# The first layer's two attentions: from 32 units of one kind each to 16 steps of one unit of each kind

## Chip, core and metric

The kernel runs on one core of one Trainium2 chip. The metric is the device time of one execution in microseconds (us), the median of several runs. The engines are called PE (TensorE; PEld is its weight load), DVE (VectorE), ACT (ScalarE), POOL (GpSimd) and SP (SyncE, which here only issues DMAs).

## What is computed

Two transformer blocks on one sequence of 512 tokens of 1024 features. The change touches the first one: two of its four mixers, and the second part of its modulation.

```python
# differential attention, 4 heads, two score maps of 32 features each ("kind A")
s = einsum('bqhcd,bkhcd->bhcqk', q, k) * 32 ** -0.5
p = softmax(s, axis=-1)
a = p[:, :, 0] - lam * p[:, :, 1]
o = rmsnorm(einsum('bhqk,bkhd->bqhd', a, v), subln_g) * (1.0 - lam_init)
# neighbourhood attention, 4 heads of 64 features, biased window + context ("kind B")
p = softmax(concatenate([s_win + bias, s_ctx], axis=-1), axis=-1)
# modulation: silu(c) @ ada_w + ada_b; four of the six parts are needed only behind the attentions
x = x + g1 * (concatenate([a_out, b_out, pool_out, hyena_out], axis=-1) @ w_out)
```

Both attentions have 512 queries (4 tiles `t` of 128) and 768 keys (256 of the context, 512 of the sequence), all in float32.

## The kernel before

The program is written engine by engine. `plan()` lists every PSUM product in the order in which PE makes it, with its banks; a product's banks are waited for (`fill`), its end is counted (`done`, waited for by `ready`), and its reader frees its first bank (`bank_free`, waited for by `read`). Each engine works through its own list in the order in which the code is written, so any wait holds back all that is written behind it. Weight tiles of 512 KB go through a ring of 12 slots; SP loads them in the order of use, each as soon as the slot's last reader has counted (`begun`, or `mod_read` for a tile of the modulation).

The attentions are one stage between the mixers' projections (`projections`) and the output product (`first_out`, `w_out`). `UNITS` are 32 units: first 16 of kind A (head by head, tile by tile), then 16 of kind B. For unit `i`, PE makes scores (L961), 6 transposes of the probabilities (L981) and 6 products with the values (L989, "PV"; values as weights, 64 columns, probabilities moving). DVE takes the row maxima (L1915, for B the bias first, L1914), the reciprocal of the row sums (L1931), normalises the probabilities (L1934 to L1938), copies the result of the unit before (L1923, `take_o`), and adds one term of the second modulation, a ring tile times a column of `silu(c)` (`mod_terms`, L1742 and L1748; 32 terms, one with each unit). ACT takes the exponentials with their sums (L1499) and copies the transposed probabilities (L1419). Scores have two pairs of banks in turn (0 and 1, 2 and 3); those of unit i+1 stand before the transposes of unit i.

Ahead of the first unit DVE prepares masks, bias and lambda (L1886 to L1905). Behind the last unit stand the 32 products that sum the modulation over the partitions (L997), and the norm of kind A's heads over all tokens (L1004, L1411, L1414, L1947).

Of the kernel before, what the change touches and what calls it, by code (L numbers as in the profile page):

```python
# [14 lines left out]
P = 128  # L15
# [163 lines left out]
def plan():  # L179
# [21 lines left out]
    r["mod2"] = b.take(7)  # L201
    b.order -= 1
    pair = 0
    for i in range(-1, len(UNITS)):
        if i + 1 < len(UNITS):
            r["scores", i + 1] = []
            for _ in range(2 if UNITS[i + 1][0] == "A" else 1):
                r["scores", i + 1].append(b.take(2 * pair, 2 * pair + 1))
                pair = 1 - pair
        if i >= 0:  # L210
            r["T", i] = [b.take(4), b.take(5)]
            r["PV", i] = b.take(6)
    r["mod2"].order = b.order
    b.order += 1
    r["subln"] = [b.take(4), b.take(5)]

    r["before_w_out"] = b.settle()
# [46 lines left out]
UNITS = [(a, h, t) for a in "AB" for h in range(HEADS) for t in range(ST)]  # L264
# [32 lines left out]
for _name, _n in (("ms_x", 1), ("ms_c", 1), ("subln", 2), ("ms_2", 1), ("ms_f", 1), ("ms_ab", 2), ("qk_ms", 10),  # L297
                  (("ffn_ms", 0), 2), ("ms_ret", 2), (("ffn_ms", 1), 1)):
    _made += _n
    ROOTS[_name] = _made  # L300


MIXED_1 = 4
MIXED_2 = MIXED_1 + 4


def two_blocks(nc, d):
# [5 lines left out]
    with ExitStack() as ctx:  # L313
# [65 lines left out]
        unused_row = tiny[:, 425:426]  # L379

# [36 lines left out]
        o_a = piece(arena, 8192, 2, S)  # L417
        prob = piece(arena, 9216, 2, 2, NKEY)
        prob_t = piece(arena, 12288, 2, NKT, P)
        raw_a = piece(arena, 13824, 4, S)  # L420
        prob_sq = piece(arena, 13824, 2, S)
        sub_rs_t = arena[:, 14848:15872]
        acc2 = piece(h_flat, D, 4, TILE)
        pool_u = piece(arena, 9216, 2, S + 16)
# [77 lines left out]
        mod_read = sem("modulation_tiles_read")  # L502
        done = sem("products_done")
# [18 lines left out]
        max_ready, exp_ready, prob_ready = sem("max_ready"), sem("exp_ready"), sem("prob_ready")  # L522
        bias_set, lam_arg, lam_exp = sem("bias_set"), sem("lam_arg"), sem("lam_exp")
        sub_sq = sem("o_a_squares")
# [85 lines left out]
        def _(sp):  # L610
# [3 lines left out]
            def read_by(t):  # L614

                if t < mod1_end:
                    return mod_read, t + 1
                if t < mod2:
                    return begun, t - mod1_end + 2
                if t < mod2_end:  # L620
                    return mod_read, 16 + t - mod2 + 1
                return begun, t - mod1_end - 32 + 3

            def load(n):

                if n >= RING:
                    sem_, value = read_by(n - RING)
                    sp.wait_ge(sem_, value)
                sp.dma_start(ring[:, n % RING, :], d["weights"][n]).then_inc(landed[n % RING], 16)

            def stream(first, last):

                turns = (last - first) // RING
                if turns:
                    with sp.Fori(0, turns) as it:
                        for s in range(RING):
                            n = first + s
                            sem_, value = read_by(n - RING)
                            sp.wait_ge(sem_, it * RING + value)
# [45 lines left out]
        def _(pool):  # L685
# [10 lines left out]
            pool.dma_start(dft, d["dft_half"]).then_inc(dft_in, 16)  # L696

# [56 lines left out]
        def _(pe):  # L754
# [192 lines left out]
            def attentions():  # L947
                def scores(i):
                    kind, h, t = UNITS[i]
                    for c, p in enumerate(r["scores", i]):  # L950
                        fill(p)
                        if kind == "A":
                            o, n, q, k = 64 * (h % 2) + 32 * c, 32, aq, ak
                            if i == 0 and c == 0:
                                pe.wait_ge(roped, 4)
                                read(pe, r["ak"][3])
                                read(pe, r["ak"][1])
                        else:
                            o, n, q, k = 64 * (h % 2), 64, bq, bk
                        for at, width in ((0, 512), (512, 256)):  # L960
                            m = pe.matmul(wide(p, NKEY)[:, at:at + width], q[o:o + n, h // 2, t * P:(t + 1) * P],  # L961
                                          k[o:o + n, h // 2, at:at + width], start=True, stop=True)
                            if i == 0 and c == 0 and at == 0:
                                begin(m)
                        finish(p, m)

                read(pe, r["bq"][1])
                for j in range(4):
                    read(pe, r["bk"][j])
                for j in range(NKT):  # L970
                    read(pe, r["v"][j])
                fill(r["mod2"])
                scores(0)
                for i, (kind, h, t) in enumerate(UNITS):
                    if i + 1 < len(UNITS):
                        scores(i + 1)
                    pe.wait_ge(prob_ready, i + 1)
                    for j, p in enumerate(r["T", i]):
                        fill(p)
                        for kt in range(4 * j, min(4 * j + 4, NKT)):  # L980
                            m = pe.transpose(ps[:, p.bank, (kt % 4) * P:(kt % 4 + 1) * P], prob[:, i % 2, 0, kt * P:(kt + 1) * P], ident)  # L981
                        finish(p, m)
                    p = r["PV", i]
                    fill(p)
                    o = DH * (h % 2)
                    for kt in range(NKT):
                        if kt % 4 == 0:
                            read(pe, r["T", i][kt // 4])
                        m = pe.matmul(ps[o:o + DH, p.bank, 0:P], vals[:, kt, 0 if kind == "A" else 1, h * DH:(h + 1) * DH],  # L989
                                      prob_t[:, i % 2, kt, :], start=(kt == 0), stop=(kt == NKT - 1))  # L990
                    finish(p, m)

                p = r["mod2"]
                for i in range(32):
                    if i % 8 == 0:
                        pe.wait_ge(mod_read, 16 + i + 8)
# [4 lines left out]
                for c, p in enumerate(r["subln"]):  # L1001
                    fill(p)
                    pe.wait_ge(sub_sq, 1)
                    finish(p, pe.matmul(bank(p), head_ones, prob_sq[:, c], start=True, stop=True))  # L1004

            def first_out():
                for b, v in r["before_w_out"]:
                    pe.wait_ge(bank_free[b], v)
                pe.wait_ge(mixed, MIXED_1)
                for i in range(8):  # L1010
# [386 lines left out]
        def _(act):  # L1397
# [91 lines left out]
            def attentions():  # L1489
# [3 lines left out]
                unit = [0]  # L1493

                def exps(i):
                    for c, p in enumerate(r["scores", i]):
                        unit[0] += 1
                        act.wait_ge(max_ready, unit[0])
                        act.activation(prob[:, i % 2, c], wide(p, NKEY), ACT.Exp, bias=neg_max[:, i % 2, c:c + 1],  # L1499
                                       accum_out=row_sum[:, i % 2, c:c + 1]).then_inc(bank_free[p.bank], 1)  # L1500

                exps(0)
                for i in range(len(UNITS)):
# [1245 lines left out]
```

## Time and profile before

| | before |
|---|---|
| median of 3 runs | 2761.19 us (2760.93 to 2763.34) |
| profiled execution, its own time | 2758.17 us |
| span of its profile | 2756.0 us |
| PE busy | 2551.9 us (93%) |
| DVE / ACT / POOL busy | 966.8 / 527.0 / 65.1 us |
| last product before the attentions to first product of `w_out` | 335.48 to 549.98 us of the span |

The span is the time between the first and the last record of the profile; the time of an execution holds some 2 us more. A busy share is an average over stages with different limits: this program is serial from stage to stage, so the stage of the attentions is read by itself. A float32 product shows as two records of PE. "idle before <-releaser" in a row says how long the engine stood still before it, and who ended that.

### The profile page before, as it was taken

How to read it: one execution, taken by the hardware profiler on the slowest of the kernel's cores; microseconds unless marked ns; L12 is line 12 of the kernel's file. 1: busy time of each engine (PE TensorE's matmuls, PEld its weight loads, DVE VectorE, ACT ScalarE, POOL GpSimd, SP SyncE). 2: the span in 40 equal slices, each digit the busy share in tenths (PEclk: the TensorE clock that was granted, in tenths of full speed). 3: DMA queues.
4: the chain of work that ended last, by engine and by line, in shares of the span. 5: the costliest groups of instructions: out<-in, count | busy, mean ns of one | idle time of the engine just before them, and what ended most of it. 6: DMA issues, size and time to landing. Idle time of an engine off the chain costs nothing.

```text
span 2756.0 us, 31092 instructions
## 1 busy us (share of the span) xinstructions
PE 2551.9 (93%) x11540; PEld 1924.5 (70%) x11540; DVE 966.8 (35%) x1743; ACT 527.0 (19%) x1095; POOL 65.1 (2%) x163
## 2 busy tenths in 40 slices
PE   7999977787999996977989999989999989899999
PEld 3565455546888884864778888847657668788888
DVE  7231277522000003126253443333323443534432
ACT  2200043321112113154121110012122110221100
POOL 1000000000111110000000000000000000000000
PEclk9999978896999997987999999999999999999999
DMA  9202123105999894210222222221211202222221
GB/s 328 99 8 62 54 72 90 54 0 193 331 329 333 327 329 179 69 31 1 62 69 77 91 79 75 91 100 54 82 48 53 76 24 105 79 92 85 84 82 63
DMA packets 83346, 307.12 MB, mean 111 GB/s; under 512 B 9264, under 2 KB 9264, under 8 KB 82624
## 3 DMA queue, kind: packets, MB, share of 16 engines
q1 hardware_dynamic: 75888, 274.24, 29.7%
q0 software_dynamic: 7376, 31.77, 2.9%
q8 instruction: 55, 0.90, 0.1%
q14 instruction: 27, 0.22, 0.0%
HBM read 292.86 MB, written 13.11 MB: 111 GB/s over the span
## 4 chain that ended last, share of the span: by engine, by line
PE 87%; DVE 7%; ACT 3%; issue 2%; DMA 1%; SPq 0%; DVEq 0%; POOL 0%; ACTq 0%; POOLq 0%
PE products L1197 37%; PE products L788 12%; PE products L1078 9%; PE products L942 7%; PE products L1090 4%; PE products L989 2%; PE products L961 2%; PE products L1323 2%; PE products L1267 1%; PE products L852 1%; PE products L896 1%; PE products L906 1%; PE products L803 1%; PE products L1181 1%; PE products L1311 1%
## 5 line engine op out<-in xcount | busy, mean ns | idle before, releaser
L1197 PE MATMUL products<-normed,ring 128*128 128x264 f32 (+1 forms) x1312 | 303.9, 388 | 11.3 <-DVE normed L2289 11.3
L1197 PEld LDWEIGHTS products<-normed,ring 128*128 128x128 f32 x1312 | 252.1, 193 | 56.1 <-issue 16.0
L1419 ACT ACTIVATE arena<-products 128x264 f32<-128x264 f32 (+3 forms) x263 | 118.6, 468 | 729.8 <-PE products L788 203.0
L1078 PEld LDWEIGHTS products<-arena,ring 128*128 128x128 f32 x2176 | 248.3, 194 | 8.8 <-issue 8.8
L1078 PE MATMUL products<-arena,ring 128*128 128x128 f32 x2176 | 248.6, 277 | 0.8 <-ACT arena L1534 0.8
L788 PE MATMUL products<-normed,ring 128*128 128x264 f32 (+2 forms) x736 | 219.7, 462 | 3.5 <-DVE normed L1726 3.5
L788 PEld LDWEIGHTS products<-normed,ring 128*128 128x128 f32 x736 | 141.6, 193 | 81.5 <-issue 65.6
L942 PE MATMUL products<-ring,normed 128*128 128x512 f32 (+1 forms) x416 | 182.5, 599 | 8.4 <-DVE normed L1726 8.4
L1197 PE MATMUL products<-arena,mixed 128*128 128x256 f32 (+1 forms) x832 | 189.4, 382 | 0.0
L1197 PEld LDWEIGHTS products<-arena,mixed 128*128 128x128 f32 x832 | 158.1, 190 | 23.8
L1197 PE MATMUL products<-normed,mixed 128*128 128x264 f32 (+1 forms) x704 | 161.5, 383 | 0.0
L1197 PE MATMUL products<-arena,normed 128*128 128x264 f32 (+1 forms) x704 | 155.6, 383 | 0.0
L942 PEld LDWEIGHTS products<-ring,normed 128*128 128x128 f32 (+1 forms) x416 | 73.7, 178 | 115.8 <-issue 115.8
L1197 PEld LDWEIGHTS products<-normed,mixed 128*128 128x128 f32 x704 | 133.8, 190 | 20.5
L1197 PEld LDWEIGHTS products<-arena,normed 128*128 128x128 f32 x704 | 133.8, 190 | 20.5
L2078 DVE TENSOR_TENSOR arena<-products,arena 128x512 f32<-128x512 f32 x17 | 11.7, 691 | 371.1 <-PE products L1078 371.1
L1197 PE MATMUL products<-arena,ring 128*128 128x256 f32 (+1 forms) x544 | 121.1, 382 | 1.6 <-DVE arena L2436 1.4
L1090 PE MATMUL products<-ring,arena 128*128 128x512 f32 x272 | 121.3, 599 | 0.0
L788 PE MATMUL products<-mixed,ring 128*128 128x264 f32 (+1 forms) x384 | 114.2, 460 | 6.2 <-DVE tiny L1952 5.3
L1197 PEld LDWEIGHTS products<-arena,ring 128*128 128x128 f32 x544 | 103.2, 190 | 18.0 <-DVE arena L2436 1.8
L788 PEld LDWEIGHTS products<-mixed,ring 128*128 128x128 f32 x384 | 73.5, 192 | 47.5 <-issue 39.3
L989 PE MATMUL products<-arena 128*64 128x128 f32 x384 | 62.8, 328 | 38.4 <-DVE arena L1923 20.3
(424 smaller groups left out, 2827.9 us busy)
## 6 DMA issues: line engine op xcount, KB each, us to landing
ring<-in_weights SPq DMA_DIRECT2D x303, 512.0 KB, 4.1
ring<-in_experts SPq DMA_DIRECT2D x204, 512.0 KB, 5.0
arena<-results SPq DMA_DIRECT2D x8, 512.0 KB, 7.6
residual<-in_x POOLq DMA_DIRECT2D x1, 2048.0 KB, 16.2
arena<-in_dft_half POOLq DMA_DIRECT2D x1, 2048.0 KB, 8.4
token_rows<-arena SPq DMA_DIRECT2D x4, 512.0 KB, 2.9
out<-residual SPq DMA_DIRECT2D x8, 256.0 KB, 4.6
arena<-in_bias POOLq DMA_DIRECT2D x1, 1920.0 KB, 24.5
```

The lines of the kernel that those rows point to most:

```text
L788: m = pe.matmul(bank(p, n), w[:, k, :], acts[:, k, at:at + n], start=(k == 0), stop=(k == kt - 1))
L803: m = pe.matmul(bank(p, n), ones, sq[:, k, at:at + n], start=(k == 0), stop=(k == KT - 1))
L852: m = pe.matmul(bank(p), w[:, c, tt, :], filt[:, tt, :, 0, :] if c == 0 else diff[:, tt], start=(tt == 0), stop=(tt == ST - 1))
L896: m = pe.matmul(ps[:, p.bank, c * 256:(c + 1) * 256], dft[:, c, tt, kt * P:(kt + 1) * P], sig_t[:, tt], start=(tt == 0), stop=(tt == ST - 1))
L942: m = pe.matmul(ps[0:n_tok, p.bank, :], acts(k), w[k // 2][:, k % 2, :], start=(k == 0), stop=(k == KT - 1))
L961: m = pe.matmul(wide(p, NKEY)[:, at:at + width], q[o:o + n, h // 2, t * P:(t + 1) * P], k[o:o + n, h // 2, at:at + width], start=True, sto ...
L989: m = pe.matmul(ps[o:o + DH, p.bank, 0:P], vals[:, kt, 0 if kind == "A" else 1, h * DH:(h + 1) * DH], prob_t[:, i % 2, kt, :], start=(kt = ...
L1078: m = pe.matmul(ps[:, side, m_ * P:(m_ + 1) * P], w[:, k, :], job_t[:, k, :], start=(k == 0), stop=(k == KT - 1))
L1090: m = pe.matmul(ps[:, 4 + half, :], hid[:, k, :], ring[:, s, half * 512:(half + 1) * 512], start=(k == 0), stop=(k == 3))
L1197: m = pe.matmul(bank(p, n), left(k), right(k), start=(fresh and k == 0), stop=(k == kt - 1), skip_group_check=True)
L1323: m = pe.matmul(ps[:, p.bank, at:S], ret_v[0:n, t, i * P:(i + 1) * P], ret_s[0:n, t, at:S], start=(t == 0), stop=(t == 4), skip_group_chec ...
L1419: act.activation(out, src, ACT.Copy, scale=scale).then_inc(bank_free[p.bank], 1)
```

## The change

The units are regrouped in 16 steps `(t, h)`. Step `s` holds the unit of kind A for head `h` and the unit of kind B for head `h ^ 1`, so that the scores of A read rows 0-63 of the array (two maps of 32 rows) and those of B rows 64-127, or the other way round. Kind A's two score maps lie side by side in banks 0, 1 and 2, kind B's in 3 and 4, transposes in 5 and 6, PV in 7: each has one set instead of two in turn. PV now has the probabilities as weights and the values moving, so that its result is token-major, 128x64; ACT copies it out and multiplies by the reciprocal row sum on the way, so that DVE no longer normalises kind B and combines kind A in one operation. The head norm is done tile by tile (`head_squares`, `roots`, `head_norm`) and the result transposed by PE (`feature_major`). The odd terms of the second modulation go to POOL, in two operations each, a product and a sum. DVE's preparation stands before the pool mixer's last products. The host stacks the modulation tiles in the new order of use.

```diff
+    scores(0, "A")
+    scores(0, "B")
+    for s in range(len(STEPS)):
+        scores(s + 1, "A")
+        scores(s + 1, "B")
+        turned(s, "A")
+        weighed(s - 1, "B")
+        turned(s, "B")
+        weighed(s, "A")
+        if s in OUT_AT:
+            r["OT", OUT_AT[s]] = [b.take(5), b.take(6)]
...
-UNITS = [(a, h, t) for a in "AB" for h in range(HEADS) for t in range(ST)]
+STEPS = [(t, h) for t in range(ST) for h in range(HEADS)]
+OUT_AT = {HEADS * t + 5: t for t in range(ST - 1)}
...
 SP, read_by:
-                    return mod_read, 16 + t - mod2 + 1
+                    j = t - mod2
+                    return (mod_added, j // 2 + 1, RING // 2) if j % 2 else (mod_read, 16 + j // 2 + 1, RING // 2)
...
 POOL:
+            ready(pool, r["scores", 0, "A"])
+            for j in range(1, 32, 2):
...
+                    pool.tensor_scalar(mod_term, w, silu_c[:, k, 0:1], None, ALU.mult).then_inc(mod_scaled, 1)
+                    pool.wait_ge(mod_scaled, j // 2 - part + 2)
+                    pool.tensor_tensor(acc2[:, part], acc2[:, part], mod_term, ALU.add).then_inc(mod_added, 1)
+                pool.wait_ge(mod_added, j // 2 + 1)
...
 PE, scores of kind A:
+                        for c, at, key, width in ((0, 0, 0, 512), (1, NKEY, 0, 256), (1, 1024, 256, 512), (0, 512, 512, 256)):
+                            rows_ = slice(o + 32 * c, o + 32 * c + 32)
+                            if at == 512:
+                                pe.wait_ge(half_scored, s + 1)
...
 PE, weigh:
-                        m = pe.matmul(ps[o:o + DH, p.bank, 0:P], vals[:, kt, 0 if kind == "A" else 1, h * DH:(h + 1) * DH],
-                                      prob_t[:, i % 2, kt, :], start=(kt == 0), stop=(kt == NKT - 1))
+                        m = pe.matmul(ps[:, p.bank, 0:DH], prob_t[:, a, kt, :], vals[:, kt, a, h * DH:(h + 1) * DH],
+                                      start=(kt == 0), stop=(kt == NKT - 1))
...
 PE, order of a step, and behind the last:
+                    scores(s + 1, "A")
+                    scores(s + 1, "B")
+                    turn(s, "A")
+                    if s > 0:
+                        weigh(s - 1, "B")
+                    turn(s, "B")
+                    weigh(s, "A")
...
+                pe.wait_ge(mod_read, 16 + 16)
+                pe.wait_ge(mod_added, 16)
...
+                feature_major(ST - 1)
...
 ACT:
+                for s in range(len(STEPS)):
+                    turned(s, "A")
+                    if s > 0:
+                        weighed(s - 1, "B")
+                    exps(s + 1, "A")
+                    turned(s, "B")
+                    exps(s + 1, "B")
+                    weighed(s, "A")
+                    if s % HEADS == 0 and s > 0:
+                        roots(s // HEADS - 1)
+                    if s in OUT_AT:
+                        feature_major(OUT_AT[s])
+                weighed(len(STEPS) - 1, "B")
+                roots(ST - 1)
+                feature_major(ST - 1)
...
 DVE:
+                def joined(s):
+                    read(dve, r["scores", s, "A"])
+                    link(dve.reciprocal(inv[:, 0:2], sums[:, 0:2]))
+                    link(stt(inv[:, 1:2], inv[:, 1:2], neg_lam, sums[:, 0:1], ALU.mult, ALU.mult))
+                    stt(prob_a[:, 0], prob_a[:, 1], inv[:, 1:2], prob_a[:, 0], ALU.mult, ALU.add).then_inc(prob_ready, 1)
...
+                for s in range(len(STEPS)):
+                    joined(s)
+                    if s in OUT_AT:
+                        head_norm(OUT_AT[s])
+                    maxima(s + 1, "A")
+                    if s % HEADS == 0 and s > 0:
+                        head_squares(s // HEADS - 1)
+                    mod2_term(2 * s)
+                    read(dve, r["scores", s, "B"])
+                    dve.reciprocal(row_inv[:, s % 2, 2:3], row_sum[:, s % 2, 2:3]).then_inc(inv_b, 1)
+                    maxima(s + 1, "B")
+                head_squares(ST - 1)
+                head_norm(ST - 1)
```

On PE this is one inner unit of kind A before (`arena` holds queries, keys, values and probabilities, `products` the PSUM banks; 128x512 and 128x256 are scores):

```order
L961 MATMUL products<-arena 128x512
L961 MATMUL products<-arena 128x256
L961 MATMUL products<-arena 128x512
L961 MATMUL products<-arena 128x256
L981 MATMUL products<-const_sb,arena 128x128 x6
L989 MATMUL products<-arena 64x128 x6
```

And this is the first part of an inner step on PE after the change, with the semaphores that each row waits for (`bank_free_0` is freed by the exponentials of kind A, `bank_free_3` by those of kind B, 5 and 6 by ACT's copies of the transposes, 7 by ACT's copy of PV):

```order
L1002 MATMUL products<-arena 128x512 [waits bank_free_0]
L1002 MATMUL products<-arena 128x256
L1002 MATMUL products<-arena 128x512
L1002 MATMUL products<-arena 128x256 [waits bank_of_both_score_halves_written]
L1010 MATMUL products<-arena 128x512 [waits bank_free_3]
L1010 MATMUL products<-arena 128x256
L1023 MATMUL products<-const_sb,arena 128x128 [waits bank_free_5,prob_ready]
L1023 MATMUL products<-const_sb,arena 128x128 x3
L1023 MATMUL products<-const_sb,arena 128x128 [waits bank_free_6]
L1023 MATMUL products<-const_sb,arena 128x128
L1034 MATMUL products<-arena 128x64 [waits bank_free_5,bank_free_7]
```

The scores of both kinds of step s+1 (L1002 and L1010) now stand before kind A's transposes of step s (L1023), with the wait for kind B's bank between them; behind the last row come kind B's transposes and kind A's PV.

On ACT, the same step after the change (128x64 is a copy of PV, 128x768 an exponential, 128x512 and 128x256 are copies of transposes):

```order
L1493 ACTIVATE arena<-products 128x512 [waits products_done]
L1493 ACTIVATE arena<-products 128x256 [waits products_done]
L1493 ACTIVATE arena<-products,tiny 128x64 [waits products_done,row_inverse_b]
L1575 ACTIVATE arena,tiny<-products,tiny 128x768 [waits max_a]
L1575 ACTIVATE arena,tiny<-products,tiny 128x768
L1493 ACTIVATE arena<-products 128x512 [waits products_done]
L1493 ACTIVATE arena<-products 128x256 [waits products_done]
L1575 ACTIVATE arena,tiny<-products,tiny 128x768 [waits max_b]
L1493 ACTIVATE arena<-products,tiny 128x64 [waits products_done]
```

Before, ACT's list for a unit held only the two copies of transposes and then the exponentials of the next unit. Now the exponential of kind B, which frees bank 3, stands behind those of kind A and behind the copies of kind B's transposes.

## Rows read from the trace of the kernel before

**Rows 1.** The page of the profile: the chain that ended last, by engine.

```profile
PE 87%; DVE 7%; ACT 3%; issue 2%; DMA 1%; SPq 0%; DVEq 0%; POOL 0%; ACTq 0%; POOLq 0%
```

**Rows 2.** Windows around and in the stage; columns as in their first line.

```profile
core 0: us, PE busy (x) PEld busy (x) DVE busy (x) ACT busy (x) POOL busy (x), PEclk, DMA share, GB/s
...
345.00:445.00 100.00, 76.97 (x392) 53.49 (x393) 80.59 (x127) 41.38 (x94) 0.00 (x0) 0.79 0.26 77
...
460.00:532.00 72.00, 53.74 (x320) 37.14 (x319) 54.01 (x86) 28.39 (x60) 0.00 (x0) 1.00 0.27 81
```

**Rows 3.** Timeline of the stage's start: us, us long, engine, line, operation.

```profile
336.54 1.61 DVE L1882 TENSOR_SCALAR mixed<-products,small 128x512 f32<-128x512 f32 x2 [30.52 <-PE products L936]
...
338.62 1.65 PE L961 MATMUL products<-arena 32*128 32x512 f32 x8 [1.25 <-DVE mixed L1882]
...
345.40 1.82 DVE L1915 TENSOR_REDUCE tiny<-products 128x1 f32<-128x768 f32 x2
```

**Rows 4.** Timeline of one unit of kind A at full clock.

```profile
360.71 0.17 DVE L1931 RECIPROCAL tiny<-tiny 128x2 f32<-128x2 f32 x1
...
360.90 1.56 PE L961 MATMUL products<-arena 32*128 32x512 f32 x8
...
361.76 1.02 DVE L1936 SCALAR_TENSOR_TENSOR arena<-arena,tiny 128x768 f32<-128x768 f32 x1
...
362.69 1.81 DVE L1915 TENSOR_REDUCE tiny<-products 128x1 f32<-128x768 f32 x2
362.83 0.64 PEld L981 LDWEIGHTS products<-const_sb,arena 128*128 128x128 f32 x6 [0.77 <-DVE arena L1936]
...
363.52 0.87 ACT L1419 ACTIVATE arena<-products 128x512 f32<-128x512 f32 x2 [2.92 <-PE products L981]
364.28 0.91 ACT L1499 ACTIVATE arena<-products,tiny 128x768 f32<-128x768 f32 x1
...
364.62 1.27 DVE L1748 SCALAR_TENSOR_TENSOR normed<-ring,tiny,normed 128x1024 f32<-128x1024 f32 x1
...
364.75 1.52 PE L989 MATMUL products<-arena 128*64 128x128 f32 x12 [1.05 <-DVE arena L1923]
...
365.94 0.22 ACT L1499 ACTIVATION_READ_ACCUMULATOR arena<-products,tiny 128x1 f32 x1
...
366.26 0.17 DVE L1931 RECIPROCAL tiny<-tiny 128x2 f32<-128x2 f32 x1 [0.37 <-ACT arena L1499]
```

**Rows 5.** The chain that ended last, through one unit of kind B.

```profile
466.20 1.52 PE products L989 x12
467.72 1.50 PE products L961 x4
...
469.25 0.71 DVE products L1914
...
471.18 1.52 PE products L989 x12
```

**Rows 6.** Timeline of the stage's end.

```profile
531.37 1.28 ACT L1411 ACT_TABLE_LOAD   x1
...
531.70 9.33 PE L997 MATMUL products<-const_sb,normed 128*128 128x1 f32 x64
...
549.98 10.25 PE L788 MATMUL products<-mixed,ring 128*128 128x512 f32 x19 [5.32 <-DVE tiny L1952]
```

**Rows 7.** The chain that ended last, in kind A where the granted clock was lower.

```profile
382.73 2.55 PE products L989 x12
385.28 2.10 PE products L961 x8
```

**Rows 8.** Groups by line and shape: ACT, then POOL. Columns: busy us, mean ns.

```profile
L1419 ACT ACTIVATE arena<-products 128x256 f32<-128x256 f32 x32 | 12.1, 378 | 0.0
...
L704 POOL TENSOR_TENSOR tiny<-const_sb 128x1 f32<-128x1 f32 x71 | 13.9, 196 | 220.8 <-PE products L1064 217.6
```

More of the change, by code:

```diff
@@ L198, in plan, with scores, turned, weighed @@
         r[name] = b.many(n)
[L201 to L217, printed above, removed]
+    def scores(s, kind):
+        if s < len(STEPS):
+            r["scores", s, kind] = b.take(0, 1, 2) if kind == "A" else b.take(3, 4)
+    def turned(s, kind):
+        r["T", s, kind] = [b.take(5), b.take(6)]
+    def weighed(s, kind):
+        if s >= 0:
+            r["PV", s, kind] = b.take(7)
+    scores(0, "A")
[10 more added lines that the diff above has]
+    weighed(len(STEPS) - 1, "B")
+    r["mod2"] = b.take(0)
+    r["OT", ST - 1] = [b.take(5), b.take(6)]
+    b.turn = 1
     r["w_out"] = b.many(8)
@@ new lines, in turn @@
+                def turn(s, kind):
+                    of = prob_a[:, 0] if kind == "A" else prob_b
+                    if kind == "A":
+                        pe.wait_ge(prob_ready, s + 1)
+                    else:
+                        read(pe, r["scores", s, "B"])
+                    for j, p in enumerate(r["T", s, kind]):
+                        fill(p)
+                        for kt in range(4 * j, min(4 * j + 4, NKT)):
+                            m = pe.transpose(ps[:, p.bank, (kt % 4) * P:(kt % 4 + 1) * P], of[:, kt * P:(kt + 1) * P], ident)
+                        finish(p, m)
@@ L1000, in attentions @@
                 tile_no[0] += 32
[L1001 to L1004, printed above, removed]
+                feature_major(ST - 1)
             def first_out():
-                for b, v in r["before_w_out"]:
-                    pe.wait_ge(bank_free[b], v)
                 pe.wait_ge(mixed, MIXED_1)
+                for p in r["pool_w"] + r["OT", ST - 1]:
+                    read(pe, p)
                 for i in range(8):
@@ new lines, in roots, with feature_major @@
+                def roots(t):
+                    act.wait_ge(sub_sum, t + 1)
+                    act.activation(sub_ln, sub_ms, ACT.Ln, bias=eps, scale=1.0 / DH).then_inc(sub_logs, 1)
+                    act.wait_ge(sub_logs, t + 1)
+                    act.activation(sub_rs, sub_ln, ACT.Exp, scale=-0.5).then_inc(sub_root, 1)
+                def feature_major(t):
+                    for a, p in enumerate(r["OT", t]):
+                        copy(p, mix[:, 2 * a:2 * a + 2, t * P:(t + 1) * P], bank(p, 2 * P).rearrange("p (c q) -> p c q", c=2),
+                             sub_g if a == 0 else 1.0)
```

262 lines of the change are left out of this document (146 added, 116 removed).

## Prediction

> **What bounds the kernel now.** I read the page first: its chain [rows 1] lies almost wholly on PE, and the program goes from stage to stage, so what this stage loses or gains passes on to the end. The windows [rows 2] then show that the stage of the attentions is different: PE is busy for 76.97 of 100 us among kind A's units and 53.74 of 72 us among kind B's, DVE for 80.59 and 54.01. Neither is full, so I read single units.
>
> A unit of kind A at full clock [rows 4] lasts from one reciprocal (360.71) to the next (366.26), 5.55 us. DVE's rows there, with the two small ones between them, come to 5.3 us with gaps of some 0.03 us: DVE bounds kind A. A unit of kind B [rows 5] lasts from 466.20 to 471.18, 4.98 us, and its chain goes round: PV, scores, DVE's bias, its maxima and its copy of the last PV, which PE waits for before it may write the bank again. DVE and PE take turns. The granted clock is 0.79 over kind A and 1.00 over kind B [rows 2]. With slower units at the low clock (PV 2.55 us for 1.52, scores 2.10 for 1.56 [rows 4, 7]) the 32 units take from 345.40 [rows 3] to about 531.8, the start of the modulation's products [rows 6]: 186 us, or 11.65 us for a pair of one A and one B.
>
> At the start PE's first scores begin at 338.62, but DVE takes up their maxima only at 345.40, behind its preparation [rows 3]. At the end 18.3 us pass from 531.70 to `w_out`'s first product at 549.98: 9.33 us of modulation products, then sums, two roots with a table load each, and two DVE operations [rows 6].
>
> **The start.** DVE stood idle 30.52 us before the pool mixer's last two operations [rows 3], which hides the 7 us of preparation once it stands ahead of them; if it were not hidden, it would cost what it cost before. The first scores still wait for those operations and start at 338.6. They end at 340.3, the maxima (one operation over 2x768; two cost 1.81 [rows 4]) at 342.1, the two exponentials (1.88 us from the first start to the accumulator's end [rows 4]) at 344.0. Step 0 has no PV of the step before; its probabilities are ready at 345.6, transposed and copied at 348.4, and the exponentials of A in step 1 end at 350.3.
>
> **An inner step.** Call e the end of kind A's exponentials of a step. Work per step, from [rows 4, 5, 8]:
> DVE: reciprocals and a small operation 0.50, join 1.02, maxima of A 1.81, modulation term 1.27, bias 0.70, maxima of B 0.91, eight gaps 0.25: 6.5 us, and 0.25 for the tile's head norm (three operations of 256 columns in four steps, estimated from the 768-column rows). 6.75 us.
> ACT: two pairs of copies 0.87 each, exponentials 1.88 and 1.0, two PV copies of 0.25 each (below the 0.378 us of the 256-column copy): 5.1 us.
> PE: scores 1.56 and 1.50, transposes 0.64 twice, PV twice. PV now loads 128 columns of weights instead of 64 and moves 64 instead of 128. No row has that shape; the transposes' weight loads go at 0.64/6 = 0.107 us each, the old PV at 1.52/12 = 0.127. I take 0.107, as loads will set the pace: 1.28 us. The upper end, the modulation products' 9.33/64 = 0.146 us at a mixed clock [rows 6], gives 1.75. Sum: 6.9 us.
>
> So no engine needs more than 6.9 us. But one set of banks for each kind ties them into a ring. From e, ACT first copies kind B's transposes (0.87), then takes kind B's exponential (1.0): bank 3 is free at e+1.9. PE made the scores of A at e+0.1 to 1.6 meanwhile; those of B start only now, so **the scores of the two kinds do not run side by side** in an inner step, whatever rows they use. They end at e+3.4. Behind them in PE's queue stand kind A's transposes, though their probabilities have been ready since e+1.5: done at e+4.0; PV of B at e+5.3, seen by ACT at e+5.6. ACT's copy of PV stands before the next exponentials of A: those run from e+5.8 to e+7.7. **7.7 us for a pair at full clock**, with DVE idle for 1 us and PE for 0.8.
>
> At the low clock this ring gets longer by 0.6 to 1.3 (scores of B), 0.3 (transposes) and 0.9 (PV): near 10 us [rows 4, 7]. PE would be busy 90% of a step, more than in either half now, of which the less busy, B, kept 1.00; but kind A's 32-row scores, which went with 0.79, stay. I take the middle, 0.90: a fifth of the time at low clock, 8.15 us a step. The ends are 7.7 and 8.7.
>
> **The tiles' ends.** Three times ACT loads two tables (1.28 each [rows 6]) and takes two short functions of 0.2: 3.0 us, from e+2.2 to e+5.2, where its next copy is due at e+4.1. That copy and the PV copy slip, the exponentials by about 0.5: 1.5 us for the three. Without the slack in the ring they would cost 9.
>
> **POOL's terms.** Nothing in the trace shows POOL on such a tile. Below, a product and a sum cost no less than DVE's two-input row, 1.27 us; above, POOL has about 8 us for a term, since it takes the odd tiles one for each step. DVE can run ahead by six tiles, the half of the ring that POOL holds; SP's queue loads in order, so a late term of POOL holds back DVE's tiles too, and PE's products wait for all 16 sums. At 3 us a term, between those ends and nearer the DVE row, all of it is hidden. The Trainium skill (GPSIMD Engine Reference, section 3.1) gives 4497 ns for an addition of 2048 float32 a partition against VectorE's 2293; by that estimate a term would be 3 to 4 us, and the sum would not change. No run here shows it yet.
>
> **The end of the stage.** After the last e (step 15) DVE's join is ready at e+1.6; transposes, PV of B, transposes, PV of A, PV of B follow on PE without a wait: e+6.7. The modulation's 64 records take 6.9 us at 0.107 and took 9.33 with the clock falling; I take 8.0. The last tile's head norm (copies, squares, 3.0 us of roots) ends before that. Four transposes, their lag and two copies of 0.38 add 1.5: `w_out` starts at e+16.2.
>
> **Sum.** 350.3 + 14 x 8.15 = 464.4 for the e of step 15, + 1.5 + 16.2 = 482.1, where it was 549.98. That is 68 us less. Nothing behind it changes. The profiled execution's 2758.17 us would become 2690; against the median of 2761.19, 3 us above it, **2693 us**. The ends of 7.7 and 8.7 us move this by 6.3 and 7.7 us; with 1.5 either way for PV's price and the end, the forecast's own range is 2685 to 2703. **0.68.**
>
> **Rivals.**
> *The scores do overlap, or ACT's order costs less than I think* (kind B's exponential done soon after e). Then DVE's 6.75 us bounds the step: 14 x 1.4 = 20 us less, 2673. For it: DVE did bound kind A. Against: the place of kind B's exponential in ACT's queue. **0.09.**
> *DVE and POOL hold each other up at SBUF.* If each of DVE's two two-input operations on SBUF in a step (1.02 and 1.27 us) waits for one operation of POOL, at least 1.27 us long, DVE needs 6.75 + 2.54 = 9.3 us and becomes the bound: 14 x 1.15 = 16 us more, 2709. It decides only past the 1 us that DVE idles in a step, and needs POOL busy at each such moment. **0.12.** The Trainium skill (SBUF — State Buffer, on the shared port pair) says just this of a DVE operation with two SBUF inputs and a reading GpSimd operation: the later one waits for the whole of the earlier. No row of before can show it, since POOL only has one-column operations there [rows 8].
> *The clock stays low throughout*, about 10 us a step: 14 x 1.85 = 26 us more, 2719. Against it stands the dense PE. **0.08.**
> *POOL is the bound and the kernel gets slower.* PE's products and what follows take 9.5 us, POOL starts at 340.3: at (550 - 9.5 - 340.3)/16 = 12.5 us a term the gain is gone; at 15 us it is 40 us slower, 2801. That is ten times DVE's row. **0.03.**
>
> **How the numbers follow.** The likeliest case gives the time. Forecast, first rival and second rival hold 0.89; the range runs from 2676, most of the first, to 2714, past the second. A measurement of this kernel can tell about 0.2% (5.5 us) from no change; all cases but the last are far beyond: faster 0.96, same 0.01, slower 0.03.
>
> **What would show it.** In the changed profile: an inner step of 7.7 us at clock 1.00; scores of B starting 1.8 us or more after those of A and right behind ACT's exponential of B; ACT's exponentials of A right behind its PV copy; DVE with some 1 us idle in a step; DVE's 1.27 us and 1.02 us rows no longer than before (else the second rival); the last POOL sum before the last PV; `w_out` near 482. I would be wrong if PE's new PV went well above 1.75 us, or if table loads or POOL stretched more than three steps.

## The result: slower, and the profile after

The changed kernel takes 2787.01 us (median of 20 runs, 2760.12 to 2793.89); the kernel before, run beside it 20 times, 2760.31 us. The ratio is 1.0085, with a 95% interval of 1.0065 to 1.0104. I had forecast 2693 us, a range of 2676 to 2714, and a chance of 0.96 for faster. The profiled execution has a span of 2784.7 us, 28.7 more than before. Ratios leave out executions recorded as slow: three of ten of "The tile's transposes moved, narrow PV" (2782 to 2785 us) and one of six of "The same with wide PV" (3709.31 us), while medians hold all.

The page of the changed kernel, parts 1 and 2:

```profile
PE 2630.6 (94%) x11552; PEld 1994.2 (72%) x11552; DVE 928.8 (33%) x1657; ACT 542.3 (19%) x1144; POOL 145.1 (5%) x193
...
PEclk9999955586999998996999999999999999999999
```

The clock's digits show it: three slices at 5, from 348 to 557 us, where the attentions are (the kernel before has 7, 8, 8 there; the 6 two slices on stood there before too). The windows of the changed kernel (columns as in the first line) answer to [rows 2]:

```profile
core 0: us, PE busy (x) PEld busy (x) DVE busy (x) ACT busy (x) POOL busy (x), PEclk, DMA share, GB/s
345.00:445.00 100.00, 99.64 (x338) 72.88 (x339) 50.72 (x63) 38.58 (x91) 60.80 (x23) 0.50 0.21 74
445.00:560.00 115.00, 115.00 (x418) 89.16 (x417) 50.45 (x72) 48.67 (x113) 15.55 (x6) 0.50 0.19 64
```

PE is busy nearly all the time, and its clock is at the lower level, 1.2 GHz, throughout; before it was 0.79 among kind A's units and 1.00 among kind B's from 460 us on. One step on PE, from the timeline of the changed kernel (it answers to [rows 4, 5, 7]):

```profile
412.17 3.37 PE L1002 MATMUL products<-arena 32*128 32x512 f32 x8
415.47 2.92 PE L1010 MATMUL products<-arena 64*128 64x512 f32 x4
418.32 1.54 PE L1023 MATMUL products<-const_sb,arena 128*128 128x128 f32 x6
419.66 2.66 PE L1034 MATMUL products<-arena 128*128 128x64 f32 x12
422.11 1.49 PE L1023 MATMUL products<-const_sb,arena 128*128 128x128 f32 x6
```

From start to start these are 3.30, 2.85, 1.34, 2.45 and 1.28 us (the second PV starts at 423.39), and a second PV of about 2.5 follows: 13.7 us, back to back. DVE's join of the steps 1, 3, 4 and 15, which now waits for ACT each time:

```profile
354.94 0.17 DVE L2038 RECIPROCAL tiny<-tiny 128x2 f32<-128x2 f32 x1 [1.97 <-ACT arena L1575]
...
383.09 0.17 DVE L2038 RECIPROCAL tiny<-tiny 128x2 f32<-128x2 f32 x1 [3.17 <-ACT arena L1575]
396.90 0.17 DVE L2038 RECIPROCAL tiny<-tiny 128x2 f32<-128x2 f32 x1 [4.34 <-ACT arena L1575]
...
551.41 0.17 DVE L2038 RECIPROCAL tiny<-tiny 128x2 f32<-128x2 f32 x1 [4.34 <-ACT arena L1575]
```

An inner step takes 13.81 us (383.09 to 396.90). The stage's end answers to [rows 6]: 

```profile
577.10 0.90 PEld L1044 LDWEIGHTS products<-const_sb,arena 128*128 128x128 f32 x4
...
578.01 0.47 ACT L1493 ACTIVATE mixed<-products,tiny 128x256 f32<-128x256 f32 x1 [10.58 <-PE products L1044]
...
579.18 2.04 PE L829 MATMUL products<-mixed,ring 128*128 128x512 f32 x2 [0.78 <-ACT mixed L1493]
```

`w_out` starts at 579.18; it was 549.98, and I had put it at 482.1. The 29.2 us between the kernels are the difference of the spans (28.7) to within 0.5 us.

### The profile page after: what moved, and what is told of

Its sections match the earlier page's. It is cut to its first block, busy times and chain, and to the rows that moved or that the text cites. A ratio compares the mean times of both kernels' runs of the same rounds, so it can differ in the third digit from the quotient of the medians.

```text
span 2784.7 us, 31110 instructions
## 1 busy us (share of the span) xinstructions
PE 2630.6 (94%) x11552; PEld 1994.2 (72%) x11552; DVE 928.8 (33%) x1657; ACT 542.3 (19%) x1144; POOL 145.1 (5%) x193
## 4 chain that ended last, share of the span: by engine, by line
PE 90%; DVE 5%; ACT 2%; issue 1%; DMA 1%; SPq 0%; DVEq 0%; POOL 0%; ACTq 0%; POOLq 0%
PE products L1271 37%; PE products L829 12%; PE products L1152 9%; PE products L983 7%; PE products L1164 4%; PE products L1034 3%; PE products L1002 2%; PE products L1397 2%; PE products L1023 2%; PE products L1010 2%; PE products L1341 1%; PE products L893 1%; PE products L937 1%; PE products L844 1%; PE products L947 1%
## 5 line engine op out<-in xcount | busy, mean ns | idle before, releaser
L2201 DVE TENSOR_TENSOR arena<-products,arena 128x512 f32<-128x512 f32 x17 | 11.7, 691 | 371.0 <-PE products L1152 371.0
L829 PE MATMUL products<-mixed,ring 128*128 128x264 f32 (+1 forms) x384 | 114.1, 460 | 1.7 <-DVE mixed L2296 0.9
L1164 PEld LDWEIGHTS products<-ring,arena 128*128 128x128 f32 x272 | 50.3, 190 | 61.0 <-issue 56.9
```

What stands on the lines that cost most here:

```text
L829: m = pe.matmul(bank(p, n), w[:, k, :], acts[:, k, at:at + n], start=(k == 0), stop=(k == kt - 1))
L1164: m = pe.matmul(ps[:, 4 + half, :], hid[:, k, :], ring[:, s, half * 512:(half + 1) * 512], start=(k == 0), stop=(k == 3))
```

## The experiments

All were timed beside the kernel before on the same chip; ratios are to it, with their 95% intervals. Theory 1 was that PV's new operand order keeps the clock low, theory 2 that the rest of the dense step does, theory 3 that POOL and DVE block one another. "Narrow" PV is the changed kernel's, with 64 moving columns; "wide" PV moves 128. The diffs show the lines that matter, cut to length.

**PV with 128 moving columns.** Same weights, the values of two heads past them, half of the result read.

```diff
-  m = pe.matmul(ps[:, p.bank, 0:DH], prob_t[:, a, kt, :], vals[:, kt, a, h * DH:(h + 1) * DH], ...
+  m = pe.matmul(ps[:, p.bank, 0:P], prob_t[:, a, kt, :], vals[:, kt, a, (h - h % 2) * DH:(h - h % 2 + 2) * DH], ...
```

> The changed kernel, but each PV product moves the values of two heads (128 columns for 64) past the same weights; 64 of the 128 result columns are read. Theory 1 (the new PV, which loads 128 columns of weights for 64 moving columns, is what keeps the clock at 0.50): the clock in the stage rises above 0.9, a step takes 7.7 to 8.7 us, the kernel about 2695 to 2710 us. Theory 2 (the clock is low because of the rest of the step, the 32-row scores and the transposes in a dense row, whatever PV does): clock 0.50, a step of 13.8 us as in the changed kernel, 2787 us.

2712.89 us, ratio 0.9813 (0.9785 to 0.9841). One edit (ACT's copy picks its half of the columns with it) turns 0.85% slower into 1.9% faster, by making PE move more. Windows of this kernel:

```profile
345.00:445.00 100.00, 92.57 (x486) 66.83 (x487) 72.82 (x89) 56.02 (x133) 75.12 (x28) 0.84 0.33 106
...
375.00:385.00 10.00, 9.84 (x64) 7.36 (x64) 9.13 (x12) 5.58 (x14) 9.72 (x4) 1.00 0.31 105
```

Theory 1 holds over theory 2, though the clock is 0.84 where it expected above 0.9, and the time 3 us above its range: the clock is 1.00 in the inner steps and falls at the tiles' ends. This kernel's joins, in inner steps at full clock and then around a tile's end:

```profile
372.45 0.17 DVE L2038 RECIPROCAL tiny<-tiny 128x2 f32<-128x2 f32 x1 [1.19 <-ACT arena L1575]
380.20 0.17 DVE L2038 RECIPROCAL tiny<-tiny 128x2 f32<-128x2 f32 x1 [0.26 <-ACT arena L1575]
387.95 0.17 DVE L2038 RECIPROCAL tiny<-tiny 128x2 f32<-128x2 f32 x1
400.34 0.15 DVE L2038 RECIPROCAL tiny<-tiny 128x2 f32<-128x2 f32 x1
411.06 0.17 DVE L2038 RECIPROCAL tiny<-tiny 128x2 f32<-128x2 f32 x1 [4.12 <-ACT arena L1575]
```

An inner step is 7.75 us at clock 1.00; the step with a tile's end takes 12.39, and the next 10.72. What holds up the tile's end in this kernel:

```profile
392.92 0.88 DVE L2051 TENSOR_TENSOR arena<-arena,tiny 128x256 f32<-128x256 f32 x1 [3.50 <-ACT tiny L1596]
...
395.51 0.90 ACT L1575 ACTIVATE arena<-products,tiny 128x768 f32<-128x768 f32 x1 [1.61 <-DVE tiny L2026]
...
398.01 0.99 PE L1044 MATMUL products<-const_sb,arena 128*128 128x128 f32 x4 [2.31 <-ACT arena L1493]
```

DVE waits 3.50 us for ACT's roots before its head norm (L2051); the maxima of kind A stand behind that in DVE's list, ACT's exponentials wait for the maxima, ACT's copies of kind B's transposes stand behind the exponentials, and PE waits for the banks that those copies free.

**PV's old operand order in the new steps**, values as weights again, results used as they lie.

```diff
+  m = pe.matmul(ps[0:DH, p.bank, 0:P], vals[:, kt, a, h * DH:(h + 1) * DH], prob_t[:, a, kt, :], ...
```

> The changed kernel with PV's operands as they were before: values as weights (64 columns), probabilities moving (128 columns). Its result then lies feature by token and is copied and used as if it were token by feature, so the attention part of the output is not the reference's; durations are those of the full work. Theory 1: clock above 0.9 and about 2700 us, as in the run with wide PV. Theory 2: clock 0.50 and 2787 us or a little more, since the old form took 2.55 us for one product set at low clock and the new one 2.66.

2716.86 us, ratio 0.9832 (0.9802 to 0.9861), clock 0.88 from 345 to 445 us and 0.92 from there to 532. 64 weight columns here, 128 in the run before, 128 moving columns in both, and the same effect: the moving side matters.

**The kernel before, with PV swapped alone.**

```diff
+  m = pe.matmul(ps[:, p.bank, 0:DH], prob_t[:, i % 2, kt, :], vals[:, kt, 0 if kind == "A" else 1, h * DH:(h + 1) * DH], ...
```

> The kernel before with PV's operands swapped alone (probabilities as weights, 64 columns of values moving); the attention result is taken from the wrong places, so the output is not the reference's. Theory 1: the clock falls to 0.5 in both halves of the stage (it was 0.79 and 1.00), and the kernel takes 30 to 60 us more than before. Theory 2: the clock stays near 0.79 and 1.00 and the time within 10 us of before, rather less, since a set of PV products gets shorter at full clock (1.28 for 1.52 us).

2828.58 us, ratio 1.0241 (1.0213 to 1.0268): 66 us more than before from this line alone. Windows of this kernel; they were at 0.79 and 0.96 in the kernel before. PE was less busy here than in the changed kernel (89.58 of 100 us for 99.64), and the clock is 0.50 all the same:

```profile
345.00:445.00 100.00, 89.58 (x320) 61.45 (x320) 65.77 (x104) 33.59 (x77) 0.00 (x0) 0.50 0.21 63
445.00:532.00 87.00, 80.29 (x258) 55.59 (x256) 47.53 (x74) 22.33 (x51) 0.00 (x0) 0.50 0.23 67
```

**POOL's terms back on DVE**, narrow PV.

```diff
   mod2_term(2 * s)
+  mod2_term(2 * s + 1)
```

> The changed kernel with POOL's 16 terms of the modulation back on DVE, two terms in each step. Theories 1 and 2: PE is the bound at 0.50, DVE idles some 7 us of each 13.8 us step and takes 1.3 us more; 2787 us within 5. Theory 3 (POOL and DVE blocking one another at SBUF costs the step): faster than the changed kernel by more than 10 us.

2788.92 us, ratio 1.01 (1.0075 to 1.0124), as the changed kernel. Theory 3 falls as the cause. One of the five executions took 2760.43 us, and that one was profiled: its clock is at 1.00 from 355 to 378 us and then falls to 0.50 for the rest of the attentions. Two windows and PE's rows of one step at full clock (L987 are kind A's scores, L1008 transposes, L1019 the narrow PV):

```profile
362.00:378.00 16.00, 15.57 (x100) 11.53 (x99) 14.64 (x20) 10.01 (x27) 0.00 (x0) 1.00 0.43 139
404.00:450.00 46.00, 46.00 (x155) 33.26 (x153) 24.43 (x32) 17.65 (x40) 0.00 (x0) 0.50 0.20 69
...
360.61 1.89 PE L987 MATMUL products<-arena 32*128 32x512 f32 x8 [0.21 <-ACT arena L1559]
...
364.62 1.45 PE L1019 MATMUL products<-arena 128*128 128x64 f32 x12
365.91 0.83 PE L1008 MATMUL products<-const_sb,arena 128*128 128x128 f32 x6
...
368.30 1.89 PE L987 MATMUL products<-arena 32*128 32x512 f32 x8 [0.21 <-ACT arena L1559]
```

With the narrow PV an inner step at full clock is 7.69 us (360.61 to 368.30) and a PV 1.29 (364.62 to 365.91). PE was busy for 15.57 of the 16 us ahead of the fall; from 378 to 388 the clock is 0.54 with PE busy for all 10 us.

**The same with wide PV.**

> Wide PV (128 moving columns), and POOL's 16 modulation terms back on DVE. With the clock up, POOL and DVE hold each other up in the wide kernel: DVE's 1.27 us term took 1.63 on average and up to 3.37. Theory A (that blocking costs more than half the terms are worth): at full clock DVE needs 6.75 + 1.3 = 8.05 us a step against the ring's 7.75, but the steps at the tiles' ends get shorter; about 2705 to 2713 us, no slower than the wide kernel (2713). Theory B (the blocking is hidden and the 1.3 us are not): 14 steps of 0.3 to 1.3 us more, 2717 to 2730 us.

2709.33 us, ratio 0.9815 (0.9791 to 0.9838); wide PV with POOL had 0.9813. No difference that can be told for the kernel. The first tile's end is shorter, as theory A had it (10.73 and 7.29 us for 12.39 and 10.72), and some inner steps are longer (8.53 for 7.75).

**The finished tile's transposes moved**, wide PV. They go from the end of step 5 into step 6, between PV of B and kind B's transposes, on PE, on ACT and in `plan()`.

```diff
-OUT_AT = {HEADS * t + 5: t for t in range(ST - 1)}
+OUT_AT = {HEADS * t + 6: t for t in range(ST - 1)}
...
                     if s > 0:
                         weigh(s - 1, "B")
+                    if s in OUT_AT:
+                        feature_major(OUT_AT[s])
                     turn(s, "B")
                     weigh(s, "A")
-                    if s in OUT_AT:
-                        feature_major(OUT_AT[s])
```

> Wide PV, and the transposes of a finished tile one step later and between PV of B and kind B's transposes, on PE, ACT and in the banks' plan. In the wide kernel the step at a tile's end takes 12.4 us for 7.75, PE idles 2.3 us or more in it, and the clock then falls to 0.5 for a step of 10.7. If the late transposes cause both: 3 x (4 + some 3) us less, about 2693 us. If ACT's table loads or POOL's blocking cause them: at most 5 us less, 2708 to 2713.

2699.55 us, ratio 0.978 (0.9756 to 0.9804): 13 us better than wide PV alone, less than the 20 expected (the intervals of the two ratios overlap a little, the executions, 2692 to 2702 and 2704 to 2718 us, do not). The step with the first tile's roots is 7.74 us, the one that now holds the transposes 8.8 (394.27 to 403.04), and the clock is 1.00 from 385 to 465. The edit does two things, though: `OUT_AT` also places DVE's head norm, which stands one step later too, and DVE's wait of 3.50 us for the roots is gone with PE's wait of 2.31 us for the banks, at all three inner tiles' ends. How the 13 us divide between the two was not tried. This kernel's timeline also shows POOL and DVE blocking one another:

```profile
386.98 1.02 DVE L2040 SCALAR_TENSOR_TENSOR arena<-arena,tiny 128x768 f32<-128x768 f32 x1
...
394.73 3.20 DVE L2040 SCALAR_TENSOR_TENSOR arena<-arena,tiny 128x768 f32<-128x768 f32 x1
394.77 2.34 POOL L736 TENSOR_TENSOR normed<-normed 128x1024 f32<-128x1024 f32 x1
```

The join with two SBUF inputs takes 3.20 us instead of 1.02 when POOL's sum of 2.34 us starts within 0.04 us of it, and PE then waits 0.32 us for the join. The Trainium skill (SBUF — State Buffer, section Who interferes with whom) says that a DVE instruction with two SBUF inputs contends with a GpSimd instruction that reads SBUF, and that the one that issues second is blocked for the whole of the first: the trace agrees, 3.20 us being near the sum of 2.34 and 1.02.

**Wide PV for kind B alone.**

> The changed kernel with wide PV for kind B alone, kind A's stays at 64 moving columns. If moving columns raise the clock by degrees: between the two, a mean clock of 0.6 to 0.8 in the stage and 2730 to 2765 us. If any wide half is enough: as the wide kernel, 2713. If it needs all: 0.50 and 2787.

2724.57 us, ratio 0.987 (0.9845 to 0.9894), clock 0.84 from 345 to 445 us. Most of the effect with half of the change; below the interval expected for "by degrees", above that for "any half is enough".

**Kind B's exponential first**, wide PV, two buffers for B's probabilities.

```diff
                     exps(s + 1, "A")
-                    turned(s, "B")
                     exps(s + 1, "B")
+                    turned(s, "B")
```

> Wide PV, kind B's probabilities in two buffers, and ACT's exponential of B ahead of its copies of kind B's transposes. By the ring as predicted (bank 3 free at e+1.0 instead of e+1.9, the scores of B then wait only for those of A to leave PE), an inner step at full clock falls from 7.75 to 7.3 or 7.4 us, and the kernel by 3 to 6 us to about 2708. If DVE's work (6.75 us with POOL's blocking on top) is the bound instead: 7.75 as before, 2713.

2724.94 us, ratio 0.9882 (0.9857 to 0.9906): slower than wide PV alone. Inner steps at full clock stay at 7.75 us; at the first tile's end the two steps are 12.4 and 14.6 us for 12.4 and 10.7, and PE waits 6.19 us for the transposes' banks there, for 2.31. So the time at which kind B's bank comes free is not what holds up B's scores. This kernel's PE timeline:

```profile
369.88 1.89 PE L1002 MATMUL products<-arena 32*128 32x512 f32 x8 [0.16 <-ACT arena L1575]
...
371.08 0.29 PEld L1002 LDWEIGHTS products<-arena 32*128 32x128 f32 x2 [0.47 <-PE products L1002]
...
371.70 1.55 PE L1010 MATMUL products<-arena 64*128 64x512 f32 x4
...
373.19 0.87 PE L1023 MATMUL products<-const_sb,arena 128*128 128x128 f32 x6
```

Kind B's bank was free at about 370.6 (its exponential ran from 369.71 for 0.91 us), yet its scores start at 371.70, 1.82 us behind A's, when those are done.

**Kind B's scores on 32 rows**, on top of the last. Half of the contraction is left out.

```diff
-  bq[o:o + DH, h // 2, t * P:(t + 1) * P], bk[o:o + DH, h // 2, at:at + width], ...
+  bq[o:o + 32, h // 2, t * P:(t + 1) * P], bk[o:o + 32, h // 2, at:at + width], ...
```

> The kernel with wide PV, two buffers for kind B and its exponential first (2725 us), but kind B's scores contract 32 features on 32 rows instead of 64 on 64: half of the contraction is left out, the columns are the same. In every run so far kind B's scores started 1.8 us after kind A's, when those were done, even in step 0, where their banks are free. If PE cannot run a product on 64 rows beside one on 32: here they start by 1.5 us, overlap the last of A's, and an inner step falls from 7.75 by 0.3 to 0.6 us. If they simply wait in the queue for A's products to end: 1.8 us and 7.75 again.

2714.78 us, ratio 0.9841 (0.9811 to 0.987), 10 us less than the last. Its PE timeline, where kind B's bank is free in time:

```profile
376.85 1.67 PE L1002 MATMUL products<-arena 32*128 32x512 f32 x7 [0.16 <-ACT arena L1575]
...
378.05 0.69 PE L1010 MATMUL products<-arena 32*128 32x512 f32 x1
...
378.37 0.37 PE L1002 MATMUL products<-arena 32*128 32x256 f32 x1
378.59 1.02 PE L1010 MATMUL products<-arena 32*128 32x512 f32 x3
```

Now a product of B starts 1.20 us behind A's first and beside A's last (378.37), and inner steps fall to 7.07 and 7.14 us. So a product on 64 rows did not run beside one on 32 rows, and two on 32 do. The Trainium skill (TensorEngine Tiling (Array Packing), section Key Properties) says that a change of the tiling mode drains TensorE: the trace agrees.

**Extra work on 64 rows**, narrow PV.

```diff
-  for at, width in ((0, 512), (512, 256)):
+  for at, width in ((0, 512), (512, 256), (0, 512), (512, 256)):
```

> The changed kernel with its narrow PV (64 moving columns), and kind B's scores made twice over (same operands, same bank, the second overwrites the first): pure extra work, 1.5 us a step at full clock and 2.9 at half. If the clock follows how many columns move in a step, whichever product moves them, it rises above 0.8 and the kernel takes 2720 to 2745 us, less than the changed one in spite of the work. If only PV's own form decides, the clock stays at 0.50 and the kernel takes 2787 + 16 x 2.9 = 2833 us.

2826.62 us, ratio 1.0236 (1.0204 to 1.0269), clock 0.50 from 385 on. The added columns on 64 rows did nothing for the clock and cost their time.

**The same extra work on 128 rows.** What was open then: whether the rows in use make the difference, and whether PV's effect comes by degrees.

```diff
+  for at, width in ((0, 512), (512, 256)):
+      pe.matmul(wide(p, NKEY)[:, at:at + width], bq[:, h // 2, t * P:(t + 1) * P],
+                bk[:, h // 2, at:at + width], start=True, stop=True)
```

> As the run with kind B's scores made twice (narrow PV, 2827 us, clock 0.50), but the added products have all 128 rows of the array at work instead of 64; same columns, same time, and the right scores overwrite them. If the clock looks at moving columns on rows in use: it rises, and the kernel takes 2720 to 2760 us in spite of the added work. If extra moving work of any kind does nothing and only PV's form counts: 0.50 and 2827 us again.

2732.99 us (nine runs, 2713.68 to 2749.0), ratio 0.9902 (0.9871 to 0.9932): useless work of 1.5 us in every step makes the changed kernel 54 us faster. The window of this kernel, on 128 rows, from the fastest of the nine executions (an inner step at full clock is 9.18 us there):

```profile
345.00:445.00 100.00, 95.71 (x541) 66.19 (x540) 69.06 (x91) 56.13 (x133) 74.67 (x28) 0.98 0.32 106
```

The same window of the kernel with the extra work on 64 rows:

```profile
345.00:445.00 100.00, 99.65 (x314) 69.62 (x311) 46.42 (x56) 33.77 (x79) 54.71 (x21) 0.51 0.19 63
```

**96 moving columns in PV.**

> The changed kernel with 96 moving columns in PV, between 64 (0.50, 2787 us) and 128 (0.84 to 1.00, 2713 us). If the effect comes by degrees: a clock between and 2730 to 2760 us. If 64 lies just below a border: as with 128, 2708 to 2718 us, since 96 columns still cost no more than the load of the weights.

2719.75 us, ratio 0.985 (0.9817 to 0.9883), clock 0.84 from 345 to 445 us and 0.82 from there to 532: near to the kernel with 128 columns (2713 us), 2 us above the second range I had written and 10 below the first.

**The tile's transposes moved, narrow PV.** The text below calls the new place earlier; it is one step later, as above.

> The changed kernel with its narrow PV and only the earlier place for a finished tile's transposes. If moving columns decide the clock, it stays at 0.50 and the kernel within 8 us of 2787. If the idle time at the tiles' ends is what keeps the clock down, it rises and the kernel takes under 2740 us.

Inconclusive: the median of 2763.33 us meets neither expectation. The ten executions form two groups, five of 2736 to 2750 us and five of 2777 to 2785, ratio 0.9978 (0.994 to 1.0016) over seven of them. The profiled one is of the second group and has 0.50 throughout. In the first group the mean clock of the program is 0.936 to 0.942 instead of 0.923 to 0.925: the same program goes either way. The changed kernel shows it too, three of its 20 executions took 2760 to 2764 us with a mean clock of 0.929 to 0.932 for 0.919 to 0.924, and so does the kernel with its terms on DVE, whose profile above catches the fall.

**Wide PV, transposes moved, all terms on DVE.**

> Wide PV, the tile's transposes in their new place, and all 32 modulation terms on DVE. Wide PV with the terms on DVE took 2709, with the transposes moved 2700, wide PV alone 2713. If DVE's 8.05 us a step is now the bound over PE's 7.75: 2700 to 2705. If the blocking between POOL and DVE still cost something in the 2700: 2690 to 2697.

2697.29 us, ratio 0.9779 (0.9752 to 0.9806). The same as with the terms on POOL (0.978). These two are the best versions, 2.2% faster than the kernel before.

## Why the prediction was wrong

**The clock.** The step that failed is "PE would be busy 90% of a step, more than in either half now ... I take the middle, 0.90". I took a dense PE as a reason for the higher clock. PE was denser than I said, over 99%, and its clock 0.50 for 230 us. I had seen that the change gives PV half the moving columns, and priced only its weight loads. The swap alone brings the kernel before from 2762 to 2829 us; undone in the new steps it brings 2787 to 2717; with 128 moving columns it brings 2713. That the new PV is the cause is shown, by taking it away and by adding it alone.

**The step at low clock.** The rival "the clock stays low throughout" had 0.08, and its price was wrong as well: "near 10 us" and 2719 us. I lengthened my ring with rows taken where the clock changed within them [rows 7], and did not ask what PE's whole queue comes to. At half clock PE's 6.9 us a step are 13.8, and 13.81 was measured; part by part it is within 0.2 us (kind A's scores 3.30 for 3.12, kind B's 2.85 for 3.00, PV 2.45 for 2.56). This is what turned a smaller gain into a loss: 14 steps of 13.8 us are 193 us, where all 32 units took 186 before.

**The sum, term by term,** to `w_out` at 579.18 for 482.1. The joins of steps 1 and 15 stand at 354.94 and 551.41, so 14 steps took 196.5 us where I had 114.1 and 1.5 for the tiles' ends: 80.9 us. The start was late by 4.5 us (354.8 for 350.3, the clock had already fallen). From the last exponentials of A to `w_out` it took 27.9 us for 16.2, 11.7 more: 5.7 in PE's products before those of the modulation, and 5.6 in the modulation's, which took 13.6 us for my 8.0 at half clock. That makes 97.1.

**What held.** DVE's preparation was hidden: the first maxima start at 341.2 instead of 345.4. At full clock my step and my price of PV were right: where the narrow PV ran at 1.00, in the profile with the terms on DVE, a step took 7.69 us for my 7.7 and a PV 1.29 for my 1.28. The ring of waits is there as well: at the start of each such step PE waits for ACT's exponentials of kind A (0.21 us, and 0.16 with wide PV). Luck has a part in one leg. The scores of the two kinds do not run side by side, but the bank I named is only one obstacle; the mixed row counts are another, which I had not seen. In the wide kernel kind A's scores start at 380.22 and B's at 382.04, 1.82 us later (0.47 of it PE's wait for the bank that both halves of A's scores share), and ACT's exponential frees kind B's bank at 381.72, so little earlier that the leg had the length I gave it (1.9 us from the end of A's exponentials; 1.96 measured), and freeing the bank sooner changed nothing.

**The tiles' ends.** With the clock up by wide PV the forecast of 2693 us would still have been 20 us too low (2713), and the tiles' ends are most of it. I had 0.5 us for each, where the first step with one lost 4.6 and the step behind it 3.0, in which the clock had fallen. I had priced the table loads by what they delay on ACT, and had left out that DVE's head norm waits for the roots with kind A's maxima behind it in its list (3.50 us, three times), and that PE then waits for the transposes' banks (2.31 us at the first).

**The other rivals.** The blocking between DVE and POOL exists, but while PE is the bound it costs nothing that can be told (2787 us with POOL's terms, 2789 without), and with wide PV no more than the terms cost on DVE (2713 and 2709). POOL was never the bound: a term took 2.96 and 2.34 us, 5.3 together, for my 3; the groups of the changed kernel (busy us, mean ns):

```profile
L734 POOL TENSOR_SCALAR normed<-ring,tiny 128x1024 f32<-128x1024 f32 x14 | 41.4, 2958 | 63.1 <-DMA ring<-in_weights 62.4
L736 POOL TENSOR_TENSOR normed<-normed 128x1024 f32<-128x1024 f32 x14 | 32.8, 2342 | 1.2
```

The Trainium skill (GPSIMD Engine Reference, section 3.1) has 4497 ns for an addition of 2048 float32 a partition, half of which, 2.25 us, is an estimate for these 1024: the trace agrees, with 2.34.

**Open.** What exactly the clock follows. Moving work on all 128 rows raised it, the same work on 64 did not; that is as far as the runs go, and since the added products on 128 rows also load weights of full height, moving columns and weights are not told apart there. Why the kernel before had 0.79 among kind A's units, and why the same program keeps the higher clock for longer in some executions, was not tried.

## What to carry to other kernels

A busy PE is no sign of a fast PE: before swapping the operands of a product so that more weights are loaded for fewer moving columns, price the whole stage at both clocks, and at the low one by the sum of PE's products as well as by the chain through the other engines, whichever is longer. Where an operation waits for another engine, look at what stands behind it in its own engine's list. Where PE is full at 0.50, try a product that moves more columns past the same full-height weights, even if the result is thrown away. Do not count on products on different rows running side by side: here 32 beside 64 did not, 32 beside 32 did.

## What the runs showed of the hardware that I had not expected

PE over 99% busy at a granted clock of 0.50 from 345 to 560 us, and in another execution a fall from 1.00 to 0.50 near 378 us, where PE had been busy for 15.57 of the 16 us before. 768 more moving columns a step on 64 rows: clock 0.50, 2827 us; on 128 rows: 0.98 in the same window, 2733 us. A product on 64 rows started only when those on 32 other rows were done (1.8 us), one on 32 rows beside them (1.2 us). POOL's product of a tile with a column, one tensor read, took 2.96 us, longer than its sum of two tiles, 2.34.
